# Four 64x64 products at once in the delta-rule solve, and its fillers dealt anew

## The chip, the core and the metric

The kernel runs on one core of a Trainium2 chip. Times are microseconds (us) of device time for one execution. Three executions of the kernel before took 1701.33, 1702.74 and 1704.41 us; their median, 1702.74 us, is the time that a change is measured against. PE is the matrix engine, PEld its weight load, DVE the vector engine, ACT the scalar engine, POOL the general engine, SP the engine that issues most transfers. PSUM is the memory that PE writes: 8 banks of 512 fp32 columns on 128 partitions. SBUF is the working memory.

## The reference

One token sequence (512 tokens, width 1024, all fp32) goes through two blocks. The first is an RWKV-7 mixer beside a stick-breaking attention. The second begins with a gated delta rule (GDN) mixer and ends with a mixture of experts. The change lies in the GDN mixer (and touches nothing else), of which this is the core:

```python
def _gated_delta_rule(q, k, v, beta, g):          # chunked; 8 q/k heads, 16 v heads, two directions
    gc = jnp.cumsum(g, axis=-1)
    decay = jnp.exp(jnp.where(incl, gc[..., :, None] - gc[..., None, :], -jnp.inf))
    kb = k * beta[..., None]
    lhs = eye + jnp.einsum("nbhik,nbhjk->nbhij", kb, k) * decay * (1.0 - eye)
    u = solve(lhs, v * beta[..., None])           # unit lower triangular solves
    w = solve(lhs, kb * jnp.exp(gc)[..., None])
    attn = jnp.einsum("nbhik,nbhjk->nbhij", q, k) * decay
    ...                                           # a scan over the chunks with a state per head

def _gdn_mixer(x, w_in, conv_w, a_log, dt_bias, norm_w, w_out):
    qkv, z, ab = jnp.split(x @ w_in, ...)
    qkv = jax.nn.silu(_dwconv(qkv, conv_w))       # 5 taps along the tokens
    q = _l2norm(q) * GDN_HEAD_DIM ** -0.5         # t * rsqrt(sum(t*t) + NORM_EPS)
    k = _l2norm(k)
    o = forward rule + reversed rule
    o = _rms(o) * norm_w * jax.nn.silu(z)
    return o @ w_out
```

## The kernel before, in words

Every engine has its own list of instructions, written out by hand in functions that are called in a fixed order (`@runs("tensor")` and so on). There is no scheduler: an engine works strictly in that order and waits on counters (`wait_ge(*s.act.at("name"))`) that other engines raise.

The GDN part handles one q/k head with its two v heads at a time: a first head, seven turns of a loop that is written out (`LOOPS = 7`), and a last half turn. A turn has two halves. In the scan half the four 128-token chunks of the head prepared one turn ago run through the state (`solved`, `state_products`, `state_update`, `attended`), while PE fills its waits with the projections of the next head (`project`, L1497), of which DVE makes convolution and silu (`convolve`, L2080; `silu`). In the second half, `levels` (PE L1616, ACT L1894, DVE L2236), the triangular matrices of the new head are inverted.

The inverse is built in levels 1 to 6 by doubling block size. There are 16 tiles of 128x128 (4 chunks, 2 heads, 2 directions), in two groups g = 0 and 1 of 8. A tile's two 64x64 diagonal blocks lie on partitions 0-63 and 64-127 (`HALF`), so that a group is held packed as 128 x (8x64). Each of the levels 1 to 4 does for each group: a product V = N T (PE L1638, 16 matmuls of 64x64x64, into bank 3g), an ACT copy of V to SBUF (L1902), a product T V (PE L1669, again 16, into bank 3g+2), and on DVE a tiny copy (L189), a predicated copy of the new blocks into T (L2214) and a 32x32-block transpose of T (L2219), which the next level's T V needs ("turned"). Levels 5 (`joined`) and 6 (`top`) work on other shapes.

PE's order in a level is V of group 0, V of group 1, T V of group 0, T V of group 1. PE waits for "T g level-1" ahead of V, and for ACT's "V g level" and DVE's "turned g level" ahead of T V. Fillers stand between: the z projection of the head (`z_part`, L1508, 128x256 steps; bank 4 for its first half, bank 1 for its second), and the transposes of k and v into tokens (`k_tokens` L1600, `v_tokens` L1593), which ACT copies out (`keep_v_tokens` L1854, four scaled copies for every two numbers k). On DVE the last of four convolutions (v1: four taps of 128x510 elements and a clamp), its silu, two `attention` products and the row sums of o^2 (`o_mean`) stand among the levels. `first_level` (L2231, L2234) prepares each group ahead of level 1.

The same pattern of product and copy stands in the RWKV part with half as many blocks (L742 and L743, L772 and L773; ACT L943). There, partitions 0-63 feed a product into partitions 0-63 of one bank (`straight`) and another into partitions 64-127 of the next bank (`crossed`), and the other half likewise.

The norms: PE sums squares with a matrix of ones (`norm`), DVE adds the epsilon while it copies PSUM to SBUF (`norm_eps`, L2090), ACT does Ln and Exp (`rsqrt`). `z_weighted` (L2175) multiplies silu(z) by norm_w, which is broadcast to all partitions.

## Time and profile before

| what | us |
|---|---|
| median of three executions | 1702.74 |
| the profiled execution: its time | 1707.7 |
| its span, first to last instruction | 1705.9 |
| PE busy in it | 1589.5 (93%) |
| DVE busy | 903.1 (53%) |
| ACT busy | 659.1 (39%) |
| POOL busy | 123.4 (7%) |
| the seven loop turns, from the first projection of the first (611.3) to the first output product behind the last (1213.7) | 602.4 |

The profiled execution took 5.0 us more than the median. A row of the trace's timeline has the start, the time and what was done; rows of equal instructions are merged. PE's fp32 matmuls appear as two records each, so that 16 matmuls are "x32". An end given for a merged PE row includes the last matmul's way through the array; the next row starts earlier than that.

### The profile page before, as it was taken

How to read it: one execution, taken by the hardware profiler on the slowest of the kernel's cores; microseconds unless marked ns; L12 is line 12 of the kernel's file. 1: busy time of each engine (PE TensorE's matmuls, PEld its weight loads, DVE VectorE, ACT ScalarE, POOL GpSimd, SP SyncE). 2: the span in 40 equal slices, each digit the busy share in tenths (PEclk: the TensorE clock that was granted, in tenths of full speed). 3: DMA queues.
4: the chain of work that ended last, by engine and by line, in shares of the span. 5: the costliest groups of instructions: out<-in, count | busy, mean ns of one | idle time of the engine just before them, and what ended most of it. 6: DMA issues, size and time to landing. Idle time of an engine off the chain costs nothing.

```text
span 1705.9 us, 36355 instructions
## 1 busy us (share of the span) xinstructions
PE 1589.5 (93%) x14884; PEld 993.8 (58%) x14884; DVE 903.1 (53%) x1956; ACT 659.1 (39%) x1316; POOL 123.4 (7%) x315
## 2 busy tenths in 40 slices
PE   5999999999999999999999999999999889777798
PEld 2465555655545757676767677777744545343443
DVE  1373562826534758686868686868610641111173
ACT  2162532515212655555565555555510112111123
POOL 7000010000000000000000000000000022122100
PEclk9999999999999999999999999999999989999999
DMA  9340111202102211111111111111054579999941
GB/s 352 107 103 2 49 51 28 72 0 99 57 13 77 78 51 51 51 51 51 51 51 51 51 51 51 51 51 50 2 202 169 226 275 419 421 420 421 386 155 50
DMA packets 105462, 210.93 MB, mean 124 GB/s; under 512 B 10195, under 2 KB 78136, under 8 KB 92029
## 3 DMA queue, kind: packets, MB, share of 16 engines
q1 hardware_dynamic: 99256, 197.52, 32.0%
q0 software_dynamic: 4896, 8.40, 1.3%
q10 hardware_dynamic: 1188, 3.28, 0.5%
q8 instruction: 90, 1.47, 0.4%
q14 instruction: 32, 0.25, 0.0%
HBM read 203.80 MB, written 14.81 MB: 128 GB/s over the span
## 4 chain that ended last, share of the span: by engine, by line
PE 50%; issue 12%; DVE 5%; ACT 2%; POOL 2%; DMA 1%; POOLq 0%; DVEq 0%; ACTq 0%
PE ps L1497 12%; PE ps L2536 5%; PE ps L1508 5%; PE ps L1669 4%; PE ps L1638 4%; PE ps L3119 3%; PE ps L506 2%; PE ps L1538 2%; PE ps L1519 1%; PE ps L1548 1%; PE ps L1560 1%; PE ps L1523 1%; PE ps L2933 1%; POOL yT L2883 1%; PE ps L1569 1%
## 5 line engine op out<-in xcount | busy, mean ns | idle before, releaser
L1497 PE MATMUL ps<-hT,W 128*128 128x512 f32 x512 | 233.5, 601 | 2.2 <-ACTq L95 2.2
L1497 PEld LDWEIGHTS ps<-hT,W 128*128 128x128 f32 x512 | 96.1, 192 | 101.1 <-issue 99.3
L594 PE MATMUL ps<-hT,W 128*128 128x512 f32 x288 | 143.3, 612 | 0.0
L1508 PE MATMUL ps<-W,hT 128*128 128x256 f32 x512 | 125.8, 389 | 0.0
L2080 DVE SCALAR_TENSOR_TENSOR arena<-ps,arena 128x510 f32<-128x510 f32 (+1 forms) x128 | 95.4, 746 | 14.0 <-ACT arena L1799 10.6
L1508 PEld LDWEIGHTS ps<-W,hT 128*128 128x128 f32 x512 | 92.2, 190 | 12.6
L2536 PE MATMUL ps<-W,yT 128*128 128x512 f32 x216 | 93.1, 592 | 0.9 <-ACT yT L1892 0.9
L1902 ACT ACTIVATE W<-ps 128x512 f32<-128x512 f32 x96 | 57.5, 599 | 69.1 <-PE ps L1638 30.8
L1669 PE MATMUL ps<-W 64*64 64x64 f32 x2304 | 77.2, 220 | 0.0
L1638 PE MATMUL ps<-W,arena 64*64 64x64 f32 x2048 | 68.5, 220 | 6.9 <-DVE spare L189 3.8
L1669 PEld LDWEIGHTS ps<-W 64*64 64x64 f32 x2304 | 72.8, 135 | 2.7 <-issue 2.7
L1638 PEld LDWEIGHTS ps<-W,arena 64*64 64x64 f32 x2048 | 63.2, 135 | 18.0 <-issue 18.0
L3010 ACT ACTIVATE arena<-arena 128x256 f32<-128x256 f32 x48 | 20.1, 418 | 133.5 <-DVE arena L2647 132.5
L2933 PE MATMUL ps<-W,yT 128*32 128x256 f32 x1024 | 58.1, 380 | 14.5 <-DMA W<-in_moe_w_up_dram 7.5
L2536 PEld LDWEIGHTS ps<-W,yT 128*128 128x128 f32 x216 | 40.9, 190 | 51.8 <-issue 51.8
L594 PEld LDWEIGHTS ps<-hT,W 128*128 128x128 f32 x288 | 48.5, 190 | 37.4 <-issue 32.2
L2663 DVE COPY yT<-ps 128x512 f32<-128x512 f32 x32 | 20.6, 686 | 89.0 <-PE ps L2946 89.0
L2933 PE MATMUL ps<-arena,yT 128*32 128x256 f32 x960 | 54.4, 380 | 13.4 <-DMA arena<-in_moe_w_gate_dram 6.9
L189 DVE COPY spare<-ones 128x1 f32<-128x1 f32 x152 | 21.6, 142 | 76.3 <-PE ps L1669 25.0
L506 PE MATMUL ps<-W,yT 128*128 128x512 f32 x128 | 60.9, 606 | 0.1
L2933 PEld LDWEIGHTS ps<-W,yT 128*32 128x32 f32 x1024 | 34.7, 110 | 41.0 <-issue 13.5
L2214 DVE COPY_PREDICATED W<-quad,ps 128x512 f32<-128x512 uint8 x80 | 57.6, 720 | 0.0
(543 smaller groups left out, 2896.5 us busy)
## 6 DMA issues: line engine op xcount, KB each, us to landing
W<-in_w_in_dram SPq DMA_DIRECT2D x33, 512.0 KB, 6.6
W<-in_gdn_w_in_dram SPq DMA_DIRECT2D x16, 1024.0 KB, 7.6
arena<-in_moe_w_up_dram SPq DMA_DIRECT2D x16, 1024.0 KB, 24.4
arena<-in_moe_w_down_dram SPq DMA_DIRECT2D x16, 1024.0 KB, 23.1
W<-in_moe_w_up_dram SPq DMA_DIRECT2D x16, 1024.0 KB, 24.1
W<-in_moe_w_down_dram SPq DMA_DIRECT2D x16, 1024.0 KB, 23.3
W<-in_moe_w_gate_dram SPq DMA_DIRECT2D x16, 1024.0 KB, 23.9
arena<-in_moe_w_gate_dram SPq DMA_DIRECT2D x14, 1024.0 KB, 24.4
```

The costliest lines, as they stand in the source:

```text
L506: mm = pe.matmul(ps[:, bank, :], yT[:, k, t * P:(t + 1) * P], wo1(k)[:, 512 * h:512 * h + 512], start=(i == 0), stop=(i == ND - 1))
L594: mm = pe.matmul(ps[:, 5 + i % 2, :], w[:, k, j, :], hT[:, k, :], start=(k == 0), stop=(k == ND - 1))
L1497: mm = pe.matmul(ps[:, 6 + k0 % 2, :], wg[:, k, j * P:(j + 1) * P], hT[:, k, :], start=(k == 0), stop=(k == ND - 1))
L1508: mm = pe.matmul(ps[:, 4 if t < 2 else 1, 256 * (t % 2):256 * (t % 2) + 256], hT[:, k, t * P:(t + 1) * P], wz[:, k, :], start=(k == 0), st ...
L1638: mm = pe.matmul(small(3 * g, m)[q, :], Nn[q, 2 * g + m // 4, m % 4, q], TTgc[q, g, m, :], start=True, stop=True)
L1669: mm = pe.matmul(small(3 * g + 2, m)[q, :], Tgc[q, g, m, :], Vgc[q, g, m, :], start=True, stop=True)
L1902: act.activation(Vgc[:, g, :, :].rearrange("p m t -> p (m t)"), ps[:, 3 * g, :], ACT.Copy).then_inc(*s.act.step(f"V {g} {lv}"))
L2080: link(dve.scalar_tensor_tensor(out=cv[:, j, to], in0=raw[:, of], scalar=taps[:, w, j:j + 1], in1=cv[:, j, to], op0=ALU.mult, op1=ALU.add) ...
L2214: dve.copy_predicated(TTgc[:, g, :, :].rearrange("p (c b) t -> p c b t", c=2), masked(lv), tiles4(ps[:, 3 * g + 2, :]))\
L2536: mm = pe.matmul(ps[:, 2 * t + h, :], yT[:, 4 * c + k, t * P:(t + 1) * P], ring[c % 3][:, k, 512 * h:512 * h + 512], start=(c == 0 and k = ...
L2933: mm = pe.matmul(ps[c0:c0 + m, 2 + j, 0:HID], xgT[:, b, k, c0:c0 + m], weights(b, j, lane, of)[:, k, :], start=(k == 0), stop=(k == ND - 1))
L3119: mm = pe.matmul(ps[:, b0 + h, :], xT[:, t, k, :], wpg[:, k, 512 * h:512 * h + 512], start=(k == 0), stop=(k == ND - 1))
```

## The change

PE, levels 1 to 4: the 16 matmuls of V are issued in another form. The first four tiles of a group go into bank 3g on their own half of the partitions, as before. The other four go into bank 3g+2 with the halves crossed, so that the product of partitions 0-63 comes out on partitions 64-127. The order goes round the four combinations of half in and half out. ACT copies V back in three instructions in place of one: 128x256 from bank 3g, and two of 64x256 from bank 3g+2, each to the other half.

The fillers of PE are dealt anew: `z_part(s, 2, ...)` had 3 steps in level 1 between the two V and 5 at its end; now it has 2, 1, 1 and 1 steps between the two V of levels 1, 2, 3 and 4, and 2 and 1 at the end of levels 1 and 4. `k_tokens` moves from the end of level 3 to that of level 2, `v_tokens` from the end of 2 to that of 3.

DVE: the last convolution is done in two halves, two taps before level 1 and two taps and the clamp after it. `first_level` of group 0 moves ahead of `output(3)`. Both `attention` products move behind level 5, silu of v1 behind level 2, `o_mean` behind level 3. `norm_eps` goes away (ACT's Ln reads PSUM with a bias `neps`), so do `z_weighted` (norm_w becomes a scale per partition in ACT's `keep_y`) and the second instruction of `o_mean` (scale and bias of ACT's Ln).

ACT: the copies of v tokens, the sigmoid of v1, o^2 and its rsqrt move to later places.

```diff
@@ -290,6 +291,7 @@
+        pool.memset(neps[:], NORM_EPS).then_inc(*su_pool.step())
@@ -1421,7 +1423,7 @@
-        sp.dma_start(nw, flat("gdn_norm_w_2").to_broadcast([P, P])).then_inc(ab_in, 16)
+        sp.dma_start(nw, a["gdn_norm_w_2"].flatten().rearrange("(p a) -> p a", a=1)).then_inc(ab_in, 16)
@@ -1502,8 +1504,8 @@
-                pe.wait_ge(*s.dve.at("norm eps 0", s.i))
-                pe.wait_ge(*s.dve.at("norm eps 1", s.i))
+                pe.wait_ge(*s.act.at("norm ln 0", s.i))
+                pe.wait_ge(*s.act.at("norm ln 1", s.i))
@@ -1613,6 +1615,9 @@
+        Z_MID = {1: range(0, 2), 2: range(4, 5), 3: range(5, 6), 4: range(6, 7)}
+        Z_END = {1: range(2, 4), 4: range(7, ND)}
+
@@ -1623,6 +1628,7 @@
                             pe.wait_ge(*s.dve.at(f"o {NT - 1}", s.i))
+                            pe.wait_ge(*s.act.at(f"qS {NT - 1}", s.i))
                         pe.nop().then_inc(admitted, 1)
@@ -1633,9 +1639,10 @@
                         else:
-                            for m in range(8):
-                                for q in HALF:
-                                    mm = pe.matmul(small(3 * g, m)[q, :], Nn[q, 2 * g + m // 4, m % 4, q], TTgc[q, g, m, :], start=True, stop=True)
+                            for m in range(4):
+                                for q, o in (HALF, HALF[::-1]):
+                                    pe.matmul(small(3 * g, m)[q, :], Nn[q, 2 * g, m, q], TTgc[q, g, m, :], start=True, stop=True)
+                                    mm = pe.matmul(small(3 * g + 2, m)[o, :], Nn[q, 2 * g + 1, m, q], TTgc[q, g, m + 4, :], start=True, stop=True)
                         mm.then_inc(*s.pe.step(f"V {g} {lv}"))
@@ -1655,8 +1662,6 @@
                         pe.wait_ge(*s.act.at(f"T {g} {lv}" if top else f"V {g} {lv}", s.i))
-                        if scan and lv == 1 and g == 0:
-                            pe.wait_ge(*s.act.at(f"qS {NT - 1}", s.i))
                         if not top:
@@ -1669,11 +1674,11 @@
                 if lv == 2:
+                    k_tokens(s)
+                if lv == 3:
                     v_tokens(s)
-                if lv == 3:
-                    k_tokens(s)
-                if lv == 1:
-                    z_part(s, 2, range(3, ND))
+                if lv in Z_END:
+                    z_part(s, 2, Z_END[lv])
@@ -1810,8 +1815,8 @@
         def rsqrt(s, j):
-            act.wait_ge(*s.dve.at(f"norm eps {j}", s.i))
-            link(act.activation(ctmp[j], ctmp[j], ACT.Ln), s.act)
+            act.wait_ge(*s.pe.at(f"norm {j}", s.i))
+            link(act.activation(ctmp[j], ps[:, 3 + PLACE[j], :], ACT.Ln, bias=neps[:, 0:1]), s.act, f"norm ln {j}")
             act.activation(ctmp[j], ctmp[j], ACT.Exp, scale=-0.5).then_inc(*s.act.step(f"rsqrt {j}"))
@@ -1879,8 +1884,8 @@
-            act.wait_ge(*s.dve.at("o eps", s.i))
-            link(act.activation(rsn, rsn, ACT.Ln), s.act)
+            act.wait_ge(*s.dve.at("o sums", s.i))
+            link(act.activation(rsn, rsn, ACT.Ln, scale=1.0 / P, bias=neps[:, 0:1]), s.act)
@@ -1889,7 +1894,7 @@
-            act.activation(yT[:, k, :], ps[:, 3 + e, :], ACT.Copy).then_inc(*s.act.step(f"{kind}y {e}"))
+            act.activation(yT[:, k, :], ps[:, 3 + e, :], ACT.Copy, scale=nw[:, 0:1]).then_inc(*s.act.step(f"{kind}y {e}"))
@@ -1899,17 +1904,23 @@
                     act.wait_ge(*s.pe.at(f"V {g} {lv}", s.i))
-                    act.activation(Vgc[:, g, :, :].rearrange("p m t -> p (m t)"), ps[:, 3 * g, :], ACT.Copy).then_inc(*s.act.step(f"V {g} {lv}"))
+                    if lv < LEVELS - 2:
+                        act.activation(Vgc[:, g, 0:4, :].rearrange("p m t -> p (m t)"), ps[:, 3 * g, 0:256], ACT.Copy).then_inc(*s.act.step(f"V {g} {lv}"))
+                        for q, o in (HALF, HALF[::-1]):
+                            act.activation(Vgc[q, g, 4:8, :].rearrange("p m t -> p (m t)"), ps[o, 3 * g + 2, 0:256], ACT.Copy)\
+                               .then_inc(*s.act.step(f"V {g} {lv}"))
+                    else:
+                        act.activation(Vgc[:, g, :, :].rearrange("p m t -> p (m t)"), ps[:, 3 * g, :], ACT.Copy).then_inc(*s.act.step(f"V {g} {lv}"))
                     if lv == LEVELS - 1:
...
                         act.activation(Tgc[:, g, :, :].rearrange("p m t -> p (m t)"), ps[:, (4, 7)[g], :], ACT.Copy).then_inc(*s.act.step(f"T {g} {lv}"))
-                    if g == 1 and lv == 1:
+                    if g == 1 and lv == 1 and scan:
+                        o_square(s)
+                    if g == 1 and lv == 2:
                         sigmoid(s, 3)
-                    for k in {(2, 1): (0, 1), (3, 0): (2,), (3, 1): (3, 4), (4, 0): (5,), (4, 1): (6, 7)}.get((lv, g), ()):
+                    for k in {(4, 0): (0, 1), (4, 1): (2, 3, 4), (5, 0): (5,), (5, 1): (6, 7)}.get((lv, g), ()):
                         keep_v_tokens(s, k // 2, k % 2)
-                    if g == 0 and lv == 1 and scan:
-                        o_square(s)
-                    if g == 1 and lv == 3 and scan:
+                    if g == 1 and lv == 4 and scan:
                         o_rsqrt(s)
@@ -2069,25 +2080,23 @@
-        def convolve(s, j):
+        def convolve(s, j, part=None):
             raw = ps[:, 6 + PLACE[j] % 2, :]
-            dve.wait_ge(*s.act.at(f"centre {j}", s.i))
-            for w in (1, 3, 0, 4):
+            if part != 1:
+                dve.wait_ge(*s.act.at(f"centre {j}", s.i))
+            for w in ((1, 3), (0, 4), (1, 3, 0, 4))[2 if part is None else part]:
                 off = w - TAPS // 2
...
                                               op0=ALU.mult, op1=ALU.add), s.dve, f"conv {j}" if w == TAPS - 1 else None)
-            dve.tensor_scalar(ctmp[j], cv[:, j, :], -LNCLAMP, None, ALU.max).then_inc(*s.dve.step(f"clamped {j}"))
+            if part != 0:
+                dve.tensor_scalar(ctmp[j], cv[:, j, :], -LNCLAMP, None, ALU.max).then_inc(*s.dve.step(f"clamped {j}"))
...
             dve.tensor_tensor(cv[:, j, :], cv[:, j, :], ctmp[j], ALU.mult).then_inc(*s.dve.step(f"silu {j}"))
-
-        def norm_eps(s, j):
-            dve.wait_ge(*s.pe.at(f"norm {j}", s.i))
-            dve.tensor_scalar(ctmp[j], ps[:, 3 + PLACE[j], :], NORM_EPS, None, ALU.add).then_inc(*s.dve.step(f"norm eps {j}"))
@@ -2162,17 +2171,11 @@
-            link(dve.tensor_reduce(rsn, osqr, X_AXIS, ALU.add), s.dve)
-            dve.tensor_scalar(rsn, rsn, 1.0 / P, NORM_EPS, ALU.mult, ALU.add).then_inc(*s.dve.step("o eps"))
+            dve.tensor_reduce(rsn, osqr, X_AXIS, ALU.add).then_inc(*s.dve.step("o sums"))
...
-
-        def z_weighted(s):
-            dve.wait_ge(*s.dve.at("silu z", s.i))
-            z8 = zg.rearrange("p c (e t) -> p (c e) t", e=2)
-            dve.tensor_tensor(z8, z8, repeat(nw, 8), ALU.mult).then_inc(*s.dve.step("z weighted"))
@@ -2235,13 +2238,10 @@
             if scan:
-                for g in range(2):
-                    first_level(s, g)
+                first_level(s, 1)
             else:
                 masked_qk(s)
-            convolve(s, v1)
-            scan_columns(s, scan)
-            attention(s, 0, s)
+            convolve(s, v1, 0)
             for lv in range(1, LEVELS):
@@ -2251,12 +2251,16 @@
                         dve.tensor_copy(TTg[q, 2 * g:2 * g + 2, b0, HALF[1 - d]], tiles4(ps[:, 3 * g + 2, :])[q, :, b0, :]).then_inc(*s.dve.step(f"T {g} {lv}"))
+                if lv == 1:
+                    convolve(s, v1, 1)
+                    scan_columns(s, scan)
                 if lv == 2:
+                    silu(s, v1)
+                if lv == 3 and scan:
+                    o_mean(s)
+                if lv == LEVELS - 2:
+                    attention(s, 0, s)
                     attention(s, NT - 1, s)
-                if lv == 1:
-                    silu(s, v1)
-                if lv == 2 and scan:
-                    o_mean(s)
@@ -2305,15 +2307,12 @@
-            z_weighted(s)
...
-            norm_eps(s, k_)
...
-            norm_eps(s, q_)
@@ -2321,6 +2320,7 @@
+            first_level(s, 0)
```

What moves, in the order in which the instructions stand. ACT, first loop turn, from the first copy of V at level 1: before (L1902 is the copy of V, L1879 o^2, L1804 to L1806 the sigmoid of v1, L1854 copies of v tokens), and then now (L1908 and L1910 the copy of V, L1884 o^2, L1809 to L1811 the sigmoid).

```order
L1902 ACTIVATE W<-ps 128x512
L1879 ACTIVATE arena<-arena 128x1024
L1902 ACTIVATE W<-ps 128x512
L1804 ACTIVATE arena<-arena 128x512
L1805 ACTIVATE arena<-arena 128x512
L1806 ACTIVATE arena<-arena 128x512
L1902 ACTIVATE W<-ps 128x512 x2
L1854 ACTIVATE arena<-ps,arena 128x128 x4
L1902 ACTIVATE W<-ps 128x512
L1854 ACTIVATE arena<-ps,arena 128x128 x2
```

```order
L1908 ACTIVATE W<-ps 128x256
L1910 ACTIVATE W<-ps 64x256 x2
L1908 ACTIVATE W<-ps 128x256
L1910 ACTIVATE W<-ps 64x256 x2
L1884 ACTIVATE arena<-arena 128x1024
L1908 ACTIVATE W<-ps 128x256
L1910 ACTIVATE W<-ps 64x256 x2
L1908 ACTIVATE W<-ps 128x256
L1910 ACTIVATE W<-ps 64x256 x2
L1809 ACTIVATE arena<-arena 128x512
L1810 ACTIVATE arena<-arena 128x512
L1811 ACTIVATE arena<-arena 128x512
```

Two copies a level became six, o^2 went behind the second group's copy, and the sigmoid from level 1 to level 2.

ACT again, from the copy of V of group 0 at level 4 on: before, from the k tokens (L1916) on, and now (L1927 the k tokens, L1859 copies of v tokens, L1888 the Ln of o's norm).

```order
L1916 ACTIVATE arena<-ps 128x512
L1902 ACTIVATE W<-ps 128x512
L1854 ACTIVATE arena<-ps,arena 128x128 x2
L1902 ACTIVATE W<-ps 128x512
L1854 ACTIVATE arena<-ps,arena 128x128 x4
```

```order
L1927 ACTIVATE arena<-ps 128x512
L1908 ACTIVATE W<-ps 128x256
L1910 ACTIVATE W<-ps 64x256 x2
L1859 ACTIVATE arena<-ps,arena 128x128 x4
L1908 ACTIVATE W<-ps 128x256
L1910 ACTIVATE W<-ps 64x256 x2
L1859 ACTIVATE arena<-ps,arena 128x128 x6
L1888 ACTIVATE arena<-arena,neps 128x8
L1889 ACTIVATE arena<-arena 128x8
```

Between the copies of V of level 4's two groups stood two copies of v tokens; now there are four.

DVE, first loop turn, from the second mask of q k to the last convolution: before (L2151 and L2152 `output(3)`, L189, L2231 and L2234 `first_level`, L2080 taps), and now (L2160 and L2161, L190, L2234 and L2237, L2092).

```order
L2100 TENSOR_TENSOR arena<-ps,GE 128x4x128
L2151 TENSOR_TENSOR W<-ps,arena 128x256
L2152 TENSOR_TENSOR arena<-arena,W 128x256
L2151 TENSOR_TENSOR W<-ps,arena 128x256
L2152 TENSOR_TENSOR arena<-arena,W 128x256
L189 COPY spare<-ones 128x1
L2231 COPY_PREDICATED W<-first_block,arena 64x512 x2
L2234 STREAM_TRANSPOSE W<-W 128x512
L189 COPY spare<-ones 128x1
L2231 COPY_PREDICATED W<-first_block,arena 64x512 x2
L2234 STREAM_TRANSPOSE W<-W 128x512
L2080 SCALAR_TENSOR_TENSOR arena<-ps,arena 128x511 x2
```

```order
L2109 TENSOR_TENSOR arena<-ps,GE 128x4x128
L190 COPY spare<-ones 128x1
L2234 COPY_PREDICATED W<-first_block,arena 64x512 x2
L2237 STREAM_TRANSPOSE W<-W 128x512
L2160 TENSOR_TENSOR W<-ps,arena 128x256
L2161 TENSOR_TENSOR arena<-arena,W 128x256
L2160 TENSOR_TENSOR W<-ps,arena 128x256
L2161 TENSOR_TENSOR arena<-arena,W 128x256
L190 COPY spare<-ones 128x1
L2234 COPY_PREDICATED W<-first_block,arena 64x512 x2
L2237 STREAM_TRANSPOSE W<-W 128x512
L2092 SCALAR_TENSOR_TENSOR arena<-ps,arena 128x511 x2
```

`first_level` of group 0 moved ahead of `output(3)`, and two taps stand where four stood.

## Rows read from the trace of the kernel before

**Rows 1.** Busy time by stretch: stretch, length, PE, PEld, DVE, ACT, POOL, clock, DMA.

```profile
600.00:1212.00 612.00, 600.68 (x7232) 442.21 (x7228) 461.63 (x1007) 350.65 (x739) 0.00 (x0) 1.00 0.16 50
```

**Rows 2.** PE's timeline, levels 1 to 4 of one turn: start, us, line.

```profile
839.89 1.15 PE L1638 MATMUL ps<-W,arena 64*64 64x64 f32 x32 [0.62 <-DVE spare L189]
840.97 1.56 PE L1508 MATMUL ps<-W,hT 128*128 128x256 f32 x6
842.46 1.15 PE L1638 MATMUL ps<-W,arena 64*64 64x64 f32 x32
843.44 2.10 PE L1669 MATMUL ps<-W 64*64 64x64 f32 x64
845.48 2.43 PE L1508 MATMUL ps<-W,hT 128*128 128x256 f32 x10
847.83 2.08 PE L1638 MATMUL ps<-W,arena 64*64 64x64 f32 x64
849.77 2.08 PE L1669 MATMUL ps<-W 64*64 64x64 f32 x64
851.78 1.09 PE L1593 MATMUL ps<-ident,arena 128*128 128x128 f32 x8
852.81 2.08 PE L1638 MATMUL ps<-W,arena 64*64 64x64 f32 x64
...
856.83 0.66 PE L1600 MATMUL ps<-ident,arena 128*128 128x128 f32 x4
857.41 2.08 PE L1638 MATMUL ps<-W,arena 64*64 64x64 f32 x64
...
861.47 0.45 PE L1634 MATMUL ps<-W,arena 32*32 32x32 f32 x32
```

**Rows 3.** PE's timeline in the RWKV part: straight and crossed products.

```profile
228.85 0.27 PE L742 MATMUL ps<-arena 64*64 64x64 f32 x1
...
229.33 0.22 PE L743 MATMUL ps<-arena 64*64 64x64 f32 x1
229.48 0.87 PE L714 MATMUL ps<-xtok 128*64 128x256 f32 x8
```

**Rows 4.** ACT's copy of V, from the groups by line: busy, mean ns.

```profile
L1902 ACT ACTIVATE W<-ps 128x512 f32<-128x512 f32 x96 | 57.5, 599 | 69.1 <-PE ps L1638 30.8
```

**Rows 5.** ACT's timeline: RWKV level 6, and v tokens in GDN.

```profile
248.47 0.38 ACT L946 ACTIVATE arena<-ps 64x256 f32<-64x256 f32 x1 [4.70 <-PE ps L747]
248.76 0.38 ACT L950 ACTIVATE arena<-ps 64x256 f32<-64x256 f32 x1
...
855.47 1.16 ACT L1854 ACTIVATE arena<-ps,arena 128x128 f32<-128x128 f32 x4
```

**Rows 6.** DVE's timeline in the same turn: end of the scan, and level 2.

```profile
835.86 0.42 DVE L2151 TENSOR_TENSOR W<-ps,arena 128x256 f32<-128x256 f32 x1 [0.40 <-PE ps L1560]
...
837.51 1.48 DVE L2231 COPY_PREDICATED W<-first_block,arena 64x512 f32<-64x512 uint8 x2
...
850.95 0.15 DVE L189 COPY spare<-ones 128x1 f32<-128x1 f32 x1 [1.35 <-PE ps L1669]
851.02 0.72 DVE L2214 COPY_PREDICATED W<-quad,ps 128x512 f32<-128x512 uint8 x1
851.78 0.71 DVE L2219 STREAM_TRANSPOSE W<-W 128x512 f32<-128x512 f32 x1
...
852.45 0.72 DVE L2214 COPY_PREDICATED W<-quad,ps 128x512 f32<-128x512 uint8 x1
```

**Rows 7.** DVE groups by line: the epsilon and the weighting of z.

```profile
L2090 DVE TENSOR_SCALAR W<-ps 128x512 f32<-128x512 f32 x16 | 11.1, 692 | 17.9 <-PE ps L1569 17.1
L2175 DVE TENSOR_TENSOR arena<-arena 128x1024 f32<-128x1024 f32 x8 | 9.8, 1220 | 0.0
```

**Rows 8.** PE's waits in the first head, a turn's scan and the last half turn.

```profile
579.92 1.15 PE L1638 MATMUL ps<-W,arena 64*64 64x64 f32 x32 [1.46 <-DVE W L2234]
...
826.80 1.13 PE L1519 MATMUL ps<-W,arena 128*128 128x256 f32 x4 [0.33 <-DVE W L2133]
...
1232.30 1.16 PE L1538 MATMUL ps<-arena,W 128*128 128x128 f32 x8 [0.38 <-DVE arena L2115]
```

More of the change, by code:

```diff
@@ L147, in build @@
     lnshift = sb("lnshift", [P, 1])
+    neps = sb("neps", [P, 1])
     spare = sb("spare", [P, 32])
@@ L1341, in build @@
     pcg = take(QUANT, NT, 4)
-    nw = take(P)
+    nw = take(1)
     rsn = take(8)
@@ L2338, in _ @@
         silu_z(s)
-        z_weighted(s)
         output(s, 1)
```

10 lines of the change are left out of this document (4 added, 6 removed).

## The prediction, made before the result was known

> **What bounds the kernel now.** I read the busy times by stretch first. Over 612 us that are nearly the seven turns of the GDN loop PE is busy for 600.68 us, at the full clock of 2.4 GHz (granted share 1.00), DVE for 462 and ACT for 351 [rows 1]. PE is the bound there, with 1.4 us of idleness per turn, and a change pays by what it takes from PE's list less the waits that it puts in. So the second view is PE's timeline of levels 1 to 4 in one turn [rows 2]. It runs from 839.89 to 861.47, 21.58 us, and its only marked wait is 0.62 us, for DVE, at the start. Two V take 0.97 us each (847.83 to 849.77), and so do T V. A V followed by a 128-row product takes 1.08 (839.89 to 840.97). Three z steps take 1.49 us and five 2.35, so a block of n steps costs 0.43 n + 0.20. With the 0.11 that V grows by, a block between 64x64 products costs 0.31 us beside its steps. Tokens of v cost 1.03 us, of k 0.58.
>
> **V on four tiles.** The RWKV part already issues straight and crossed 64x64 products. Sixteen of them start between 228.85 and 229.33 and are out 0.22 us later, 0.70 us in all [rows 3], where the two-tile form has a row of 1.15 [rows 2]. That is 0.45 us less, so V costs 0.52 us. The bounds are 0.48 (the starts alone) and 0.97 (no overlap gained). PE loses 8 x 0.45 = 3.6 us per turn.
>
> On this form a page speaks against the change. The Trainium skill ("TensorE: Matmul & The Clock Gate", Part 3) says that a weight load overlaps running matmuls only when its row group differs, and here every second matmul has its predecessor's rows. By that V would stay near 0.97 us; the sum goes by the 0.70 us above.
>
> **The fillers.** There were two blocks of z steps and two of tokens in these levels; now there are six and two. Four more blocks cost 4 x 0.2 = 0.8 us, and the step from V to one, 0.1 each at three more places, 0.3: together 1.1.
>
> **ACT's copies.** One copy of 128x512 (0.60 us, [rows 4]) becomes one of 128x256 and two of 64x256. A 64x256 copy from PSUM takes 0.38 us, and the next starts 0.29 behind it [rows 5]. The three end 2 x 0.285 + 0.38 = 0.95 us after they start, against 0.60. No row has a copy that changes partitions. Bounds: 0.95, and 3 x 0.41 = 1.23 if nothing overlaps; far out, 1.5 if each crossed copy costs a 512-wide one (0.29 + 2 x 0.60). I take 0.95, since every other copy from PSUM follows the one before at that pace.
>
> The Trainium skill ("TensorEngine Tiling (Array Packing)", PSUM Bottleneck) warns that after a tiling speedup the copy out of PSUM may become the bottleneck and asks for both ScalarE and VectorE. Here ACT alone pays. The next part works out from rows that this comes true in part.
>
> **Waits that come.** A V is done 0.22 us after its last issue, and a semaphore costs about 0.06. In DVE's rows of level 2 [rows 6] the tiny copy starts 0.20 us after T V of group 0 is issued (T V starts at 849.77, takes 0.98), the predicated copy 0.07 later, the transpose 0.76 later, and group 1's predicated copy starts at 852.45 and takes 0.72. So V of group 1 may start 2.48 us after T V of group 0 is issued. I call V0, V1, T0, T1 the products of the two groups.
> - T1 waits for ACT: it starts V1 + 0.52 + 0.22 + 0.95 + 0.06 = V1 + 1.75, while T0 is through at V1 + 1.50: 0.25 us of wait in each level.
> - From V1 to the next V1: 1.75 + T1 0.98 + filler at the end + V0 0.52 + 0.10 + one z step 0.63 = 3.98 us + end filler. By DVE it is 0.52 + 0.98 + 2.48 = 3.98 as well. Before it was 3.90 + fillers. So the levels keep their length, and what is won is that z steps go into them free.
>
> Start: DVE is free at 835.46 (835.86 less its 0.40 of idleness, [rows 6]). `first_level` of a group takes 0.07 + 1.45 + 0.66 = 2.2 us, `output(3)` 1.7. Now group 0 first, then the output, done at 839.36 and seen at 839.39; this is when V0 starts, in place of 839.89. Group 1 is ready at 841.59.
> - Level 1: V0 839.39, two z steps, V1 at 841.59 (0.5 of wait for DVE), T0 842.11, T1 843.34, two z steps from 844.32, to 845.38.
> - Level 2: V0 845.38, V1 846.63, T1 848.38 to 849.36, k tokens to 849.94. DVE's second half of the convolution (two taps, clamp, columns, 2.0 us from 846.3) ends at 848.3, where T0's blocks are due at 848.33: just covered.
> - Level 3: V1 851.19, T1 852.94 to 853.92, v tokens to 854.95. ACT's sigmoid (1.9 us from 848.4) is through at 850.3, and V0 is due at 850.7.
> - Level 4: V1 856.20. Between the copies of the two groups ACT now has four token copies, at 0.25 each [rows 5], as the order shows. V0 is copied from 855.69 on (0.86 until ACT is free), the tokens take to 857.55, V1's triple to 858.50, T1 starts at 858.56, 0.86 late. It ends at 859.54; one z step; level 5 starts at 860.17.
>
> The same bookkeeping for before gives 861.19 for 861.47. I compare sums with sums: 860.17 - 861.19 = -1.02 us per turn. Check: -3.6 + 1.1 + waits 2.4 (0.29 + 0.52 + 3 x 0.25 + 0.86) - waits 0.9 = -1.0. Levels 5 and 6 have ACT and DVE idle enough for the rest of the tokens (1.5 us) and the two attention products (1.5 us).
>
> **DVE relieved.** Per turn two epsilon copies of 0.69 us and a weighting of 1.22 us go [rows 7]. I cost this at nothing in the scan: its one wait, 0.33 at L1519, follows a state that DVE starts as soon as PE's product lands [rows 8]. Adding the bias in ACT's Ln costs ACT nothing that PE sees. The moved waits (q S ahead of V0, Ln ahead of z) are met long before. In the last half turn the weighting stood ahead of the residual that PE waited 0.38 us for [rows 8]: -0.4.
>
> **First head.** PE waits 1.46 us for `first_level` of group 1 there [rows 8], behind triangles that ACT's decays pace: that stays. But the convolution behind it is halved, so that level 2 starts 2.3 us earlier; of this the later levels, 10.2 us against 8.6 from level 3 on, give back most. By the same bookkeeping level 5 starts 1.6 us earlier.
>
> **Sum.** 7 x (-1.02) - 1.6 - 0.4 = -9.1 us, from 1707.7 to 1698.6 in the profiled execution. That one lies 5.0 us above the median; from the median, 1702.74 - 9.1 = 1693.6 us. Own range: V at 0.48 gives 1.9 us more; 0.05 us more on each triple takes 2 back, 0.1 takes 4; the extra wait for DVE at level 1 may vary by 0.3 a turn. 1689 to 1699.
>
> **Rivals.**
> - The copies do not overlap (1.23 us). T1 then waits 0.53 in each level and ACT's queue at level 4 feels it twice: +0.22 us per turn against before, -0.35 for the first head: 1703.5, no change. The 0.29 spacing speaks against it; that no crossing copy is in the trace speaks for it.
> - Slower: the crossed copy is dear. If it costs a 512-wide copy without overlap, the triple takes 1.5 us and every level waits for ACT: +2.1 us per turn, 1718. It decides from a triple of 1.2 us on.
> - The four tiles do not run side by side, the result of the page's rule on weight loads. V stays at 0.97 and the copies are dearer: 871.6 against 869.95 at the turn's end, +1.7, 1715. Rows 3 speak against it; their products are eight to a group, not sixteen, but of the same form.
> - Only PE's list counts, and no wait comes: -2.5 less the 0.3 of the earlier start, 8 times, and -0.4: 1680. For it speaks that PE has hardly waited so far; against it the 3.98 us, which DVE and ACT give independently.
>
> **Chances.** The measurement tells a change from none at about 0.2%, 3.4 us. Forecast 0.62 (all of it faster), only PE 0.08 (faster), copies without overlap 0.16 (0.14 the same, 0.02 slower), dear crossing 0.09 and no tiles 0.05 (slower). Faster 0.70, same 0.14, slower 0.16. The range of 8 in 10 takes in the forecast and the no-change case, 1684 to 1704, and leaves out the ends.
>
> **What would show it.** In the changed profile: V in 0.5 us and 64 of them; an ACT triple of 0.95 us with 0.29 between; PE's wait ahead of T V of group 1, 0.25 us in levels 1 to 3 and 0.9 in level 4; a wait of 0.5 ahead of the second V of level 1; about 20.8 us from level 1 to level 5, where 21.6 are now; PE busy 17 us less in the loop (7 x 2.5) and idle 10 more (7 x 1.5). The forecast is wrong if T V waits for anything but ACT, if a crossed copy takes over 0.4 us, or if the scan changes its length by more than 0.3 us a turn.

## The result, and the profile after

The changed kernel takes 1707.51 us (median of 13 runs, 1704.69 to 1710.16), the kernel before 1703.69 (13 runs): ratio 1.0024, 95% interval 1.0016 to 1.0031. It is slower by some 4 us, where 1693.6 was predicted. The profiled spans are closer, 1706.6 us against 1705.9; "Medians against spans" below takes them apart.

First the busy time by stretch (columns as in [rows 1]).

```profile
600.00:1212.00 612.00, 589.16 (x7194) 417.22 (x7194) 441.34 (x978) 387.39 (x860) 0.00 (x0) 1.00 0.16 50
```

PE is busy for 11.5 us less than in [rows 1], where the prediction had 17, and idle for 22.8 us instead of 11.3. A fixed stretch doesn't tell whether the loop got shorter. The length of a turn is best read from one instruction that comes once in each, ACT's copy of q and k at the head of level 1: from its second start to its eighth there are six turns, 667.13 to 1183.20 before and 667.30 to 1184.98 after: 86.01 and 86.28 us each. (A "turn" below is this mean.) The prediction said 1.02 less; it became 0.27 more. The change's six turns all take 86.27 to 86.30 us. Those of the kernel before do not agree: 86.27, 86.40, 86.01, 86.02, 85.78 and 85.57. Its first four have a break inside T V of level 5, in the middle of its 16 products, which the profile puts down to no other engine:

```profile
864.36 0.32 PE L1666 MATMUL ps<-W 32*32 32x32 f32 x15
864.92 0.34 PE L1666 MATMUL ps<-W 32*32 32x32 f32 x17 [0.24 <-issue]
```

The traces of the change and of its run with the old V have none in these six turns. Why the kernel before has it is not known. Against the last two turns, which have no break, the change loses 0.5 to 0.7 us and not 0.27.

Next PE's timeline of the turn that [rows 2] show, with the V products left out but for the ends of the first two. L1644 and L1645 are V, L1674 is T V, L1510 a z step, L1602 the k tokens, L1640 level 5.

```profile
839.34 0.24 PE L1644 MATMUL ps<-W,arena 64*64 64x64 f32 x1
...
839.82 0.22 PE L1645 MATMUL ps<-W,arena 64*64 64x64 f32 x1
839.96 1.13 PE L1510 MATMUL ps<-W,hT 128*128 128x256 f32 x4
841.49 0.24 PE L1644 MATMUL ps<-W,arena 64*64 64x64 f32 x1 [0.40 <-DVE W L2237]
...
842.13 1.15 PE L1674 MATMUL ps<-W 64*64 64x64 f32 x32
843.58 1.15 PE L1674 MATMUL ps<-W 64*64 64x64 f32 x32 [0.30 <-DVE spare L190]
844.65 1.13 PE L1510 MATMUL ps<-W,hT 128*128 128x256 f32 x4
...
847.81 1.15 PE L1674 MATMUL ps<-W 64*64 64x64 f32 x32
849.06 1.15 PE L1674 MATMUL ps<-W 64*64 64x64 f32 x32
850.14 0.66 PE L1602 MATMUL ps<-ident,arena 128*128 128x128 f32 x4
...
858.27 1.15 PE L1674 MATMUL ps<-W 64*64 64x64 f32 x32
860.51 0.70 PE L1674 MATMUL ps<-W 64*64 64x64 f32 x17 [1.09 <-ACT W L1910]
...
861.59 0.70 PE L1510 MATMUL ps<-W,hT 128*128 128x256 f32 x2
862.22 0.45 PE L1640 MATMUL ps<-W,arena 32*32 32x32 f32 x32
```

V does what was promised: its 16 products (32 records) start within 0.48 us (839.34 to 839.82), and the z steps follow 0.62 after V's start. It also starts where the bookkeeping had it, 839.34 for 839.39. But T V of group 1 comes at 843.58 where 843.34 was predicted, and from there each level is later than predicted, until level 5 starts at 862.22 for 860.17. Many of these waits carry no mark in the profile: T V of group 0 is issued at 847.81, takes 0.97, and T V of group 1 starts at 849.06, 0.28 after PE could.

ACT's timeline of the same levels says why. L1908 is the straight copy, L1910 the two crossed ones, L1859 the tokens.

```profile
840.80 0.38 ACT L1908 ACTIVATE W<-ps 128x256 f32<-128x256 f32 x1
841.20 0.78 ACT L1910 ACTIVATE W<-ps 64x256 f32<-64x256 f32 x2
842.24 0.38 ACT L1908 ACTIVATE W<-ps 128x256 f32<-128x256 f32 x1 [0.26 <-PE ps L1645]
842.65 0.78 ACT L1910 ACTIVATE W<-ps 64x256 f32<-64x256 f32 x2
...
856.94 0.38 ACT L1908 ACTIVATE W<-ps 128x256 f32<-128x256 f32 x1 [2.38 <-PE ps L1645]
857.35 0.78 ACT L1910 ACTIVATE W<-ps 64x256 f32<-64x256 f32 x2
858.15 1.14 ACT L1859 ACTIVATE arena<-ps,arena 128x128 f32<-128x128 f32 x4
859.16 0.40 ACT L1908 ACTIVATE W<-ps 128x256 f32<-128x256 f32 x1
859.59 0.78 ACT L1910 ACTIVATE W<-ps 64x256 f32<-64x256 f32 x2
```

Two copies of 0.38 us each take 0.78 together, and the first of them starts 0.40 to 0.41 behind the straight one. A triple thus takes 0.41 + 0.78 = 1.19 us, where 0.95 was predicted and [rows 4] show 0.60 for the one copy of before. No copy overlaps the next, while those of [rows 5] do. A crossed copy is not dear in itself: it has the 0.38 us of every other.

The two timelines also tell which wait is whose. T V starts 0.15 us behind the end of the last copy of its triple in all four levels of this turn: the copies end at 841.98 and 843.43, T V starts at 842.13 and 843.58; in level 4 they end at 860.37 and it starts at 860.51. So T V waits for ACT even where the profile says `DVE spare L190`, as at 843.58. L190 is DVE's tiny copy, which ended at 843.53 by chance; what T V needs of DVE in level 1 was written by 840.60.

### The profile page after: what moved, and what is told of

Same layout as the page of the kernel before. It is cut to its first block, busy times and chain, and to the rows that moved or that the text cites. A ratio compares the mean times of both kernels' runs of the same rounds, so it can differ in the third digit from the quotient of the medians.

```text
span 1706.6 us, 36452 instructions
## 1 busy us (share of the span) xinstructions
PE 1577.0 (92%) x14884; PEld 966.4 (57%) x14884; DVE 880.7 (52%) x1924; ACT 698.7 (41%) x1444; POOL 123.1 (7%) x316
## 4 chain that ended last, share of the span: by engine, by line
PE 42%; issue 12%; DVE 8%; ACT 6%; POOL 2%; DMA 1%; POOLq 0%; SPq 0%; DVEq 0%; ACTq 0%
PE ps L1499 12%; PE ps L2535 5%; PE ps L1674 4%; PE ps L3118 3%; PE ps L1510 3%; PE ps L508 2%; PE ps L1540 1%; DVE W L2234 1%; DVE arena L2092 1%; PE ps L2932 1%; PE ps L1644 1%; PE ps L1550 1%; PE ps L1521 1%; ACT arena L1829 1%; PE ps L1525 1%
## 5 line engine op out<-in xcount | busy, mean ns | idle before, releaser
L1510 PE MATMUL ps<-W,hT 128*128 128x256 f32 x512 | 134.7, 396 | 0.0
L2092 DVE SCALAR_TENSOR_TENSOR arena<-ps,arena 128x510 f32<-128x510 f32 (+1 forms) x128 | 95.1, 743 | 14.2 <-ACT arena L1804 11.0
L1674 PE MATMUL ps<-W 64*64 64x64 f32 x2304 | 83.7, 222 | 16.5 <-ACT W L1910 9.0
L1510 PEld LDWEIGHTS ps<-W,hT 128*128 128x128 f32 x512 | 89.8, 190 | 13.2
L1674 PEld LDWEIGHTS ps<-W 64*64 64x64 f32 x2304 | 75.6, 136 | 25.6 <-issue 25.3
L190 DVE COPY spare<-ones 128x1 f32<-128x1 f32 x152 | 22.2, 146 | 96.4 <-PE ps L1674 39.8
L3118 PE MATMUL ps<-arena,W 128*128 128x512 f32 x128 | 55.7, 593 | 0.1
L2932 PEld LDWEIGHTS ps<-arena,yT 128*32 128x32 f32 x960 | 30.1, 110 | 40.1 <-DMA arena<-in_moe_w_gate_dram 11.3
```

The costliest lines, as they stand in the source:

```text
L190: return dve.tensor_copy(spare[:, k:k + 1], ones[:, 0:1])
L1510: mm = pe.matmul(ps[:, 4 if t < 2 else 1, 256 * (t % 2):256 * (t % 2) + 256], hT[:, k, t * P:(t + 1) * P], wz[:, k, :], start=(k == 0), st ...
L1674: mm = pe.matmul(small(3 * g + 2, m)[q, :], Tgc[q, g, m, :], Vgc[q, g, m, :], start=True, stop=True)
L2092: link(dve.scalar_tensor_tensor(out=cv[:, j, to], in0=raw[:, of], scalar=taps[:, w, j:j + 1], in1=cv[:, j, to], op0=ALU.mult, op1=ALU.add) ...
L2932: mm = pe.matmul(ps[c0:c0 + m, 2 + j, 0:HID], xgT[:, b, k, c0:c0 + m], weights(b, j, lane, of)[:, k, :], start=(k == 0), stop=(k == ND - 1))
L3118: mm = pe.matmul(ps[:, b0 + h, :], xT[:, t, k, :], wpg[:, k, 512 * h:512 * h + 512], start=(k == 0), stop=(k == ND - 1))
```

## The experiments

**What decides the spacing of copies.** The changed kernel with twelve trials of copies from PSUM behind the last state of the scan; each trial is a row of copies of 256 columns, with a wait for the one before between trials.

```
+ lo, hi, al = HALF[0], HALF[1], slice(0, P)      # (source, destination)
+ trials = [[(al, al)] * 4, [(lo, lo)] * 4, [(hi, hi)] * 4,
+     [(lo, lo), (hi, hi), (lo, lo), (hi, hi)], [(hi, lo)] * 4, [(lo, hi)] * 4,
+     [(lo, hi), (hi, lo), (lo, hi), (hi, lo)], [(lo, lo), (hi, lo), ...],
+     [(lo, lo), (lo, hi), ...], [(al, al), (lo, lo), ...],
+     [(al, al), (hi, hi), ...], [(al, al), (hi, lo), (lo, hi), (al, al)]]
```

> The changed kernel with 48 extra copies on ACT in the last half turn, twelve rows of four, each a 256-column Copy from one PSUM bank to SBUF; only the partitions differ from row to row. It measures the start-to-start time of copies by itself. In the changed kernel's trace two 64x256 copies to alternating halves take 0.78 us, 0.40 apart, where I had reckoned 0.29. Theory 1 (a change of the partitions that are read or written keeps ACT from starting the next instruction before the last has ended): rows with the same partitions four times, crossed or not, have 0.29 us; rows that alternate halves, crossed or not, have 0.40. Theory 2 (crossing itself costs): the crossed rows have 0.40 also with one and the same half four times, and alternating uncrossed copies have 0.29. Theory 3 (half the partitions cost): every 64-row copy has 0.40. The time of the kernel is no matter here, some 20 us longer.

ACT's timeline of it: the start of trial 2 (lower half four times), all of trial 4 (lower and upper half in turn, nothing crossed), and from trial 5 (all four crossed, upper to lower) copies 1 and 2, then 2 and 3.

```profile
1243.21 0.65 ACT L1941 ACTIVATE arena<-ps 64x256 f32<-64x256 f32 x2
...
1245.66 0.38 ACT L1941 ACTIVATE arena<-ps 64x256 f32<-64x256 f32 x1
1246.06 0.38 ACT L1941 ACTIVATE arena<-ps 64x256 f32<-64x256 f32 x1
1246.46 0.38 ACT L1941 ACTIVATE arena<-ps 64x256 f32<-64x256 f32 x1
1246.87 0.38 ACT L1941 ACTIVATE arena<-ps 64x256 f32<-64x256 f32 x1
1247.28 0.65 ACT L1941 ACTIVATE arena<-ps 64x256 f32<-64x256 f32 x2
1247.56 0.64 ACT L1941 ACTIVATE arena<-ps 64x256 f32<-64x256 f32 x2
```

Uncrossed copies that alternate between the halves start 0.40 us apart; crossed ones that all go the same way start 0.28 apart. So it is not the crossing. Over all trials:

| copies in a row | starts apart, us |
|---|---|
| same halves: all, lower, upper, upper to lower, lower to upper | 0.26 to 0.29 |
| lower and upper in turn, nothing crossed | 0.40, 0.40, 0.41 |
| lower to upper and upper to lower in turn | 0.40, 0.41, 0.40 |
| only the source's half changes | 0.40, 0.41, 0.40 |
| only the destination's half changes | 0.40, 0.40, 0.40 |
| 128 rows and the lower 64 in turn | 0.28, 0.26, 0.26 |
| 128 rows and the upper 64 in turn | 0.41, 0.40, 0.41 |
| the change's triple and the straight copy after it | 0.41, 0.40, 0.40 |

The two rows with 128-row copies tell the rule apart from "same shape": 128 rows and the lower 64 both start at partition 0, and they overlap. A copy overlaps the one before it if source and destination start on the same partitions as that one's. If either changes, it starts 0.13 us later. The change's triple has such a step twice inside it, and a third time to the straight copy after it. This is the recorded theory 1; theories 2 and 3 fall. (The kernel took 1724.87 us, in one run.)

**The V product undone.** The changed kernel with V and its copy as before; the fillers, the split convolution and the norms' epsilon stay changed.

```
- for m in range(4):
-     for q, o in (HALF, HALF[::-1]):
-         pe.matmul(small(3 * g, m)[q, :], Nn[q, 2 * g, m, q], ...)
-         mm = pe.matmul(small(3 * g + 2, m)[o, :], Nn[q, 2 * g + 1, m, q], ...)
+ for m in range(8):
+     for q in HALF:
+         mm = pe.matmul(small(3 * g, m)[q, :], Nn[q, 2 * g + m // 4, m % 4, q], ...)
```

> The changed kernel with V of levels 1 to 4 and ACT's copy of it as before (two tiles at once, one copy of 128x512); fillers, DVE's order, the norms as changed. Theory A (the four-tile V is worth a little, the triple copies eat nearly all of it, and the new deal of fillers alone loses by its additional blocks): the bookkeeping of a turn gives +0.5 us against before, where it gives +0.2 for the changed kernel, so +3 to +4 us, 1707 to 1711. Theory B (the four-tile form is what loses, and the rest of the change gains): faster than before by 4 us or more, below 1700.

It took 1704.96 us (12 runs), ratio 1.0008 (0.9998 to 1.0018), with a turn of 86.02, the mean of before. Neither expectation has this time. In the mean the rest of the change is worth nothing in a turn: four more blocks on PE, 0.8 us more of busy time in a turn (85.2 for 84.4 by the busy share), in exchange for 0.8 less of idleness. (Its turns have no break in level 5; against the two turns of before that have none, 85.78 and 85.57, it is 0.24 and 0.45 slower, the direction of theory A.) And V on four tiles with its triple costs 0.26 us a turn in the deal of the change, where it was to save.

**The V product alone.** The kernel before, with V and its copies as in the change, and the wait for q S moved ahead of V since its bank is written earlier.

```
+ pe.wait_ge(*s.act.at(f"qS {NT - 1}", s.i))      # ahead of V 0
+ the V product and the triple of copies of the change
```

> The kernel before with the four-tile V and the three copies alone; fillers, DVE's order and the norms as before. Theory A: with the old deal ACT's sigmoid (1.9 us) and the copies of v tokens stand between the triples, and DVE's whole convolution ahead of level 1: the bookkeeping gives +1.8 us per turn, 1714 to 1720. Theory B (four-tile V loses): slower as well, but by no more than 5 us. Theory C (the new deal loses and V wins): faster than before, 1695 or less.

It took 1725.25 us (4 runs), ratio 1.0125 (1.0109 to 1.0141), its turn is 88.55 us (665.41 to 1196.68), 2.5 longer: the direction of theory A, larger than its numbers. The waits of PE in one turn (us in total, times, longest):

```profile
PE ps L1669 <- ACT W L1905: 4.2, 5, 1.3
PE ps L1669 <- DVE arena L2086: 0.5, 1, 0.5
```

L1905 are the crossed copies. With the fillers as before, no z step stands between the products in levels 2 to 4, and ACT's token copies fall between the triples: five T V wait. So the rest of the change, its deal of fillers above all, was needed, and the first shape of the answer is here: the price of a triple depends on what stands beside it.

**Two copies without a change of half.** The changed kernel with 128x256 straight from either bank. Left out: the crossing back, so half of the V products are used with the other half's rows.

```
- act.activation(Vgc[:, g, 0:4, :]..., ps[:, 3 * g, 0:256], ACT.Copy)
- for q, o in (HALF, HALF[::-1]):
-     act.activation(Vgc[q, g, 4:8, :]..., ps[o, 3 * g + 2, 0:256], ACT.Copy)
+ for bank, m0 in ((3 * g, 0), (3 * g + 2, 4)):
+     act.activation(Vgc[:, g, m0:m0 + 4, :]..., ps[:, bank, 0:256], ACT.Copy)
```

> The changed kernel in which V comes back in two copies of 128x256, one from each bank, with the same partitions in and out; left out: the crossing back of the second one, so the numbers are those of another matrix. PE, DVE and the fillers do exactly what they do in the changed kernel. It prices the third copy and the lost overlap: the pair should take 0.29 + 0.38 = 0.67 us in place of 1.18. Theory A (the triple is the bound of a level): -2.2 us per turn against before, 1684 to 1690. Theory D (DVE's chain of 3.98 us per level is the bound, the triples only lie beside it): 1702 or more, no different from the changed kernel by more than 5 us.

It took 1686.03 us (4 runs), ratio 0.9892 (0.9877 to 0.9908), with a turn of 83.50. The two copies took 0.66 us together. Half a microsecond less on ACT behind each V is worth 2.8 us a turn: ACT's copies are on the path.

**Three copies that start on the same partition.** This is the forecast's own assumption made real: as many copies as in the change, each starting at partition 0. Left out as before: the crossing back; the third copy goes to a scratch buffer.

```
- for q, o in (HALF, HALF[::-1]):
-     act.activation(Vgc[q, g, 4:8, :]..., ps[o, 3 * g + 2, 0:256], ACT.Copy)
+ act.activation(Vgc[:, g, 4:8, :]..., ps[:, 3 * g + 2, 0:256], ACT.Copy)
+ act.activation(fl(ob[HALF[0], 2 * g:2 * g + 2, :]), ps[HALF[0], 3 * g + 2, 0:256], ACT.Copy)
```

> The changed kernel with three copies behind each V product of levels 1 to 4 as before, but all three start on partition 0 in source and in destination: 128x256 of the first bank, 128x256 of the second bank uncrossed, and 64x256 of the second bank into a scratch buffer. Left out: the crossing back, so half of the V products are used with the other half's rows. Theory A (overlap needs the start partitions of the copy before; with it the triple ends 0.95 us after its start as the forecast had it, not 1.18): the copies start 0.28 us apart and the time is the forecast's, 1691 to 1697. Theory B (three copies cost what they cost by their number, and only their count matters): no difference from the changed kernel, 1705 to 1710.

It took 1695.65 us (6 runs), ratio 0.9951 (0.9932 to 0.9969). ACT's timeline of one triple:

```profile
839.03 0.38 ACT L1908 ACTIVATE W<-ps 128x256 f32<-128x256 f32 x1 [0.53 <-PE ps L1645]
839.31 0.38 ACT L1909 ACTIVATE W<-ps 128x256 f32<-128x256 f32 x1
839.58 0.37 ACT L1910 ACTIVATE W<-ps 64x256 f32<-64x256 f32 x1
```

It takes 839.95 - 839.03 = 0.92 us, and a turn 84.77: 1.24 below the kernel before, where the forecast had 1.02, and 1.51 below the change. The number of copies is the same, so what the change lost between forecast and result is the missing overlap. PE's timeline there, V and both T V of level 1:

```profile
838.28 0.24 PE L1644 MATMUL ps<-W,arena 64*64 64x64 f32 x1 [0.39 <-DVE W L2236]
838.76 1.14 PE L1674 MATMUL ps<-W 64*64 64x64 f32 x32
840.09 1.15 PE L1674 MATMUL ps<-W 64*64 64x64 f32 x32 [0.19 <-ACT W L1910]
```

T V of group 0, whose copies are done by then, follows 0.48 us behind V's start; in the change it took 0.64. And the wait ahead of T V of group 1, with nothing else changed, is now marked as ACT's.

**The token copies out of the way.** The changed kernel with the eight copies of token halves on ScalarE dealt later.

```
- for k in {(4, 0): (0, 1), (4, 1): (2, 3, 4), (5, 0): (5,), (5, 1): (6, 7)}
+ for k in {(4, 1): (0, 1, 2), (5, 0): (3, 4), (5, 1): (5, 6, 7)}
```

> The changed kernel with one thing moved: the eight copies of the token halves on ScalarE are dealt 3, 2, 3 over (level 4 group 1), (level 5 group 0), (level 5 group 1), with none before the last triple of level 4, where the change has 2, 3, 1, 2. Theory A (the triple takes 1.18 us, because a copy that starts on other partitions than the one before it gets no overlap, and in level 4 it stands behind the token copies on the way to the first T product of group 1): the wait before that T product falls from 1.09 to about 0.6 us, the turn by 0.9 us by the bookkeeping of waits, 1699 to 1703. Theory B (the copies' queue in level 4 is not what sets T's start there; the price is the four-tile product itself): no difference from the changed kernel, 1706 to 1709.

It took 1699.04 us (12 runs), ratio 0.9977 (0.9965 to 0.9989), a turn 85.28: 1.00 less than the change, where the bookkeeping with 1.18 us for a triple gave 0.9. PE's waits in a turn no longer hold the 1.1 for L1910; 0.28 us without a mark is left there (T V of group 0 starts at 857.96, of group 1 at 859.21):

```profile
PE ps L1521 <- DVE W L2142: 0.3, 1, 0.3
PE ps L1674 <- DVE spare L190: 0.3, 1, 0.3
```

(The second row is again T V of level 1, which waits for ACT, as above.) This one line keeps every result and makes the change faster than the kernel before, by 0.1 to 0.35%.

**The fillers dealt for 1.18 us.** The changed kernel, with the fillers of PE placed by the same bookkeeping once the triple is entered at its measured length: more z steps between V and V, where T V must wait, fewer at the ends; both token blocks inside level 4; ACT's other work out of levels 1 to 4 where it can go.

```
+ Z_AT = {(1, 0): (0, 3), (1, 1): (3, 4), (2, 0): (4, 6), (2, 1): (6, 7), (3, 0): (7, 8)}
+ # (level, 0 between V and V, 1 between T V and T V); v tokens at (4, 0), k tokens at (4, 1)
+ # ACT: token halves {(4, 1): (0,), (5, 0): (1, 2, 3), (5, 1): (4, 5, 6, 7)}
+ # ACT: square of o and the k tokens' copy at (4, 1), the norm's root at (5, 1)
+ # DVE: row sums of o^2 behind level 4, not 3
```

> The four-tile V product and the triple of copies as in the change, with the fillers of TensorE dealt by the bookkeeping that has 1.18 us for the triple: z blocks 3 between V0 and V1 and 1 between T0 and T1 in level 1, 2 and 1 in level 2, 1 between V0 and V1 in level 3; in level 4 the v tokens between V0 and V1 and the k tokens between T0 and T1; on ScalarE the k tokens' copy, the square of o and one token half behind level 4, the rest and the norm's root in level 5. Theory A (each turn's cost is the waits that 1.18 us of copies leave open, and fillers can close them): 2.5 us a turn below the kernel before, 1684 to 1690. Theory B (fillers only move the waits, since the recurrence through DVE and ScalarE is as long as before): 1700 to 1708.

It took 1682.97 us (5 runs), ratio 0.9876 (0.9859 to 0.9894): faster than both kernels. A turn is 83.24 us, 2.77 below the kernel before (2.5 predicted). PE in the loop:

```profile
600.00:1170.00 570.00, 562.49 (x6578) 398.84 (x6576) 427.15 (x950) 365.72 (x810) 0.00 (x0) 1.00 0.18 53
```

7.5 us idle in 570, 1.1 a turn, against 3.2 a turn after the change (22.84 / 612 x 86.28). The triple is as slow as ever (its two crossed copies have 0.78 us in every level), but its waits are filled. PE's timeline of level 4 in one turn:

```profile
843.08 1.09 PE L1595 MATMUL ps<-ident,arena 128*128 128x128 f32 x8
...
845.99 0.65 PE L1602 MATMUL ps<-ident,arena 128*128 128x128 f32 x4
846.57 1.15 PE L1681 MATMUL ps<-W 64*64 64x64 f32 x32
847.65 0.45 PE L1647 MATMUL ps<-W,arena 32*32 32x32 f32 x32
```

L1595 are the v tokens, L1602 the k tokens, L1681 T V, L1647 level 5. Both token blocks stand where PE would wait for ACT, and T V of group 1 (846.57) starts as soon as the k tokens are issued.

**The same deal with the old V.** The kernel above with the V product and the copy of before.

```
+ the deal of fillers above, V and its copy as in the kernel before
```

> The same deal of fillers as the run above with the V product and its single copy as in the kernel before (16 products into one bank, one copy of 128x512). It tells what the four-tile product itself is worth once the fillers fit. Theory A (V0 and V1 cost TensorE 0.45 us less each, and with the fillers dealt TensorE's list sets the turn): this is the kernel before within 0.2%, 1702 to 1710, some 20 us above the run above. Theory B (what gains is the deal alone): it is as fast as the run above, 1684 to 1692.

It took 1703.11 us (12 runs), ratio 0.9991 (0.9978 to 1.0004), with a turn of 85.80. The deal alone is worth 0.2 us a turn; V on four tiles in it is worth 85.80 - 83.24 = 2.56 us a turn, 18 of the 20 us between this run and the one above.

## Why the prediction was wrong

**The step that failed** is the one headed "ACT's copies": "The three end 0.95 us after they start", with the reason that every other copy from PSUM follows the one before at that pace. Measured: 1.19 us. All the copies from which the pace was taken ([rows 5]) start on the partitions of their predecessor, as the first experiment shows after the fact. The bound of 1.23 us was right, and the rival built on it, "the copies do not overlap", is what happened: it said +0.22 us a turn, and +0.27 was measured. It had a chance of 0.16. That its number came so close is in part luck: two errors that it shares with the forecast, the transition and the breaks below, offset each other. Its other number, -0.35 for the first head, was wrong, as below.

A second term of the same sum was small too: "a semaphore costs about 0.06". From ACT's last copy to T V it is 0.15 us (860.37 to 860.51). V of group 1 to its T V was put at 1.75 us and took 2.09 in levels 1 to 3: 0.24 more is the triple, 0.09 the semaphore.

The trace of before had the answer in two rows that were not looked up, since they are no copies of V:

```profile
557.04 1.18 ACT L1789 ACTIVATE arena<-ps 32x512 f32<-32x512 f32 x2
...
870.28 2.58 ACT L1861 ACTIVATE W<-W 64x512 f32<-64x512 f32 x4
```

The first are two copies of 0.59 us from different quarters that take 2 x 0.59, with no overlap. The second are four that alternate between the halves, 0.65 apart.

The Trainium skill says that back-to-back ACTIVATEs overlap by about 93 ns ("ScalarE: Activation LUTs", What ACT_TABLE_LOAD costs). The trials agree in size, 0.38 - 0.28 = 0.10 us, where the partitions stay, and disagree where they change: there nothing overlaps, and the start comes 0.02 us after the end of the copy before.

**Point by point.**
- V on four tiles costs 0.52 us: right. Its starts span 0.48, the next z steps come at 0.62 as worked out. Where T V needn't wait it follows V's start by 0.48 (838.28 to 838.76 in the run with three copies that start alike); the 0.64 of the change (841.49 to 842.13) holds a wait for ACT. One transition was missing: from T V to another form takes 1.07 (843.58 to 844.65), not 0.98, which four times a turn makes 0.4 us. The Trainium skill's rule on weight loads ("TensorE: Matmul & The Clock Gate", Part 3), by which they overlap running matmuls only when the row group differs, was read by the prediction as 0.97 for V. The measurement is against that reading.
- The start at 839.39: right (839.34). So was the wait for DVE ahead of the second V (841.49 for 841.59; marked 0.40 for 0.5).
- T V of group 1 waits for ACT, 0.25 us in each level: the place was right, the size not. It waits 843.58 - 842.13 - 0.97 = 0.48 in level 1. Group 0's T V, for which no wait was forecast, waits too: 842.13 - 841.49 - 0.52 = 0.12 in level 1 and 847.81 - 846.97 - 0.52 = 0.32 in level 2, with 0.28 for group 1 after it.
- In level 4 T V of group 1 is 0.86 late: the mechanism was right, four token copies stand ahead of the triple, and the later deal took it away (-1.00 a turn). The wait measured 860.51 - 858.27 - 0.97 = 1.27, since ACT's queue there holds two triples.
- Added up: level 5 starts 2.05 us later than predicted, 1.64 of it T V of group 1 coming late in the four levels (0.24, 0.34, 0.34, 0.72) and 0.4 the transition. Two errors went the other way. Level 5 and what follows to z's end took 871.08 - 862.22 = 8.86 us where before it took 870.76 - 861.47 = 9.29, which is the break shown above; and the bookkeeping put before's level 5 at 861.19 for 861.47. -1.02 + 2.05 - 0.43 - 0.28 is +0.32, for +0.27 measured.
- First head, -1.6: wrong. Level 5 starts there at 602.02, 1.9 us later than before (600.14), so 3.5 us are to be found. The wait for DVE ahead of V of group 1 grew from 1.46 to 2.22, since PE no longer spends itself on z and V before it, but it ends at the same time (579.97 for 579.92). Levels 2 to 4 took 16.70 us, 1.9 more than the prediction gave them, for the reasons above. And 1.1 is the clock: behind that wait PE ran at a granted share of 0.68 for 5.35 us, partly at 1.2 GHz, and did what takes 4.22 us in a turn. Before, the share was 1.00 there. Without this the first head would be about 0.75 us slower than before.

```profile
579.97 0.24 PE L1644 MATMUL ps<-W,arena 64*64 64x64 f32 x1 [2.22 <-DVE W L2237]
...
582.05 1.23 PE L1674 MATMUL ps<-W 64*64 64x64 f32 x18 [0.22 <-ACT W L1910]
...
600.31 0.88 PE L1674 MATMUL ps<-W 64*64 64x64 f32 x23 [1.09 <-ACT W L1910]
```

The stretch from V of group 1 at level 1 to V of level 2, in the first head and then in a turn, both after:

```profile
579.97:585.32 5.35, 5.13 (x101) 4.41 (x101) 5.16 (x10) 1.14 (x3) 0.00 (x0) 0.68 0.01 3
841.49:845.71 4.22, 3.92 (x100) 3.31 (x100) 3.50 (x8) 2.66 (x6) 0.00 (x0) 1.00 0.02 4
```

- DVE relieved, nothing in the scan: right, the wait at L1521 is still 0.33. Last half turn, -0.4: right. The wait of 0.38 for the residual is gone, and the half turn with the wait behind it takes 1254.70 - 1216.20 = 38.50 us, for 1252.67 - 1213.70 = 38.97.

**Medians against spans.** The medians differ by 3.8 us (2.7 to 5.3 by the interval), the two profiled spans by 0.7. Part of that is the clock, which falls in other places in the two traces. Here are the stretches behind a pause of 2.2 us in which PE waits for ACT's queue, before and then after.

```profile
611.28:616.48 5.20, 5.20 (x8) 2.19 (x9) 0.69 (x1) 0.00 (x0) 0.00 (x0) 0.67 0.30 103
```

```profile
613.15:616.66 3.51, 3.51 (x9) 1.60 (x10) 0.69 (x1) 0.00 (x0) 0.00 (x0) 1.00 0.44 149
```

The same work took 1.69 us more before, at a granted share of 0.67, that is partly at 1.2 GHz; after, it ran at 2.4. But after had its own such stretch in the first head (1.13 us, above), which before had not. At full clock the parts are: first head +0.75, seven turns 603.05 - (602.42 - 1.69) = +2.3, last half turn -0.5, together +2.6. The rest of the kernel was not changed; there the trace of before took 1.3 us more, with one more stretch of low clock (granted share 0.66 from 1638 to 1643). So the parts account for 2.6 of the 3.8 us. Where the clock fell in the executions that were not profiled, and where the rest lies, is not known.

The Trainium skill's warning that the copy out of PSUM may become the bottleneck after a tiling speedup ("TensorEngine Tiling (Array Packing)", PSUM Bottleneck) came true: in the change T V waited for ACT's copies in each of the four levels. Its advice to use ScalarE and VectorE together was not tried here; filling PE's waits was enough.

**What stays open.** Why V alone costs 2.5 us a turn (1725.25 us, where 1714 to 1720 were expected) is seen only as five marked waits and not taken apart. What stops PE in level 5 of the kernel before is unknown. Whether the deal with the most z steps between V and V is the best one was not searched on the chip: PE still idles 1.1 us a turn in it.
